# Where the additions of the decode tokens' expert rows stand in VectorE's program

## The chip, the cores and the metric

The kernel runs on one core of a Trainium2 chip. The metric is the device time of one launch in microseconds (us); less is better. Times are medians of several runs; the profile is of one execution more.

## The reference

One inference step of a small hybrid decoder (two layers, model width 1024) for two groups that share the weights: a prompt of 512 tokens and 8 decode tokens with 4096 cached positions each. Layer 0 mixes with differential attention and a gated recurrence, layer 1 with a short gated convolution. After each mixer comes the PEER block, the part that matters here:

```
def one(xb):
    q = (xb @ w_q).reshape(blk, PEER_HEADS, 2, PEER_KDIM // 2)
    s = jnp.einsum('thcd,hcnd->thcn', q, sub_keys).astype(jnp.float32)
    s1, i1 = lax.top_k(s[:, :, 0], PEER_TOPK)
    s2, i2 = lax.top_k(s[:, :, 1], PEER_TOPK)
    cand = (s1[..., :, None] + s2[..., None, :]).reshape(blk, PEER_HEADS, PEER_TOPK * PEER_TOPK)
    sc, ci = lax.top_k(cand, PEER_TOPK)
    ...
    g = jax.nn.softmax(sc, axis=-1)
    act = jax.nn.gelu(jnp.einsum('td,thkd->thk', xb, u_tab[eidx]).astype(jnp.float32))
    coef = (g * act).astype(xb.dtype)
    return jnp.einsum('thk,thkd->td', coef, v_tab[eidx])
```

For each token, 8 heads choose 16 of 128 x 128 = 16384 experts by two top-16 searches over 128 sub-keys each and one over their sums. Each chosen expert has a row in `u_tab` and one in `v_tab`; the output is added to the residual.

## The kernel before

The prompt's 512 tokens lie in four token tiles of 128; the 8 decode tokens are a fifth, `xs[0:DEC, TILES, :]`. Each engine has its own program, written out by hand, and they meet only in semaphores.

PEER is computed in three ways. The decode tokens and token tiles 2 and 3 fetch their experts' rows one by one from HBM (POOL's indirect DMAs into eight `ring` buffers). Token tiles 0 and 1 are computed densely: all 16384 experts in 128 blocks (`NCH`), and a table of gates `G`, which is zero for experts that weren't chosen. A block of gates for 8 tokens (`OT`) and 32 expert blocks (`CH`) is made by TensorE as a product of one-hot matrices: VectorE's `onehots` writes these (lines L1809, L1811 and L1816, called a one-hot group), TensorE's `gates` multiplies them (24 matmuls, L937), ScalarE copies the result into `G` (L1301). One-hot group n waits until TensorE has done gates n - 2, by two buffers.

The search for the experts is `choose`: five stages for each row (MAX8, FIND_INDEX8, MATCH_REPLACE8, MAX8, FIND_INDEX8; L1693 to L1697), for 16 score rows and then for 8 rows of sums, 120 stages in all. A list `beside` of other work is spread among them: one piece after each `every` stages, `every = (5 * 3 * nh) // (len(beside) + 1)`, with nh = 8. After the stages follow L1736 to L1788, which turn places into expert numbers and scores into gates.

In each layer VectorE calls `tile(1)` for token tile 3, then multiplies the decode tokens' fetched u rows, then `tile(2)` (token tile 0), then the additions that this change moves, then `tile(3)` (token tile 1) with one-hot groups 0 to 15 beside it, and `tile(4)` (token tile 2) with groups 16 to 31. Group 0 first waits for `indices_turned`, the copy by ScalarE (L1294, L1295) of what TensorE transposed in `turn(0)` (L927), splits the gates into three bf16 parts (`split_gates`, L1795 and L1797) and copies a table (L1880). At the end `chosen` lets TensorE and POOL into the loops over ranges of experts.

TensorE's order around this is: the last query products (L898); the decode tokens' output rows, gate-weighted sums of the fetched v rows into two PSUM banks (L990, its end is released at L994); `ahead(2)`, products of slices of the u table for the dense tiles (L949, 16 matmuls each; ScalarE's GELU of them is L1310; each slice is loaded into one of two buffers by L566); `turn(0)`; `ahead(1)`; then

```
            pe.wait_ge(dve_bank_free, nv[0])
            for n in range(CH // 2):
                gates(l * NCH + n, n, e2o0, e1o0)
                if n == SCORES_BEHIND:
                    scores(1, q2)
                if n % 4 or n < 8:
                    ahead(1)
            turn(1)
```

`dve_bank_free` counts the additions among other readers of the PSUM banks, and `gates` writes two of these banks. `SCORES_BEHIND` is 11. `turn(1)` waits for the end of `tile(3)`.

Of the kernel before, what the change touches and what calls it, by code (L numbers as in the profile page):

```python
# [22 lines left out]
ALU = mybir.AluOpType  # L23
# [7 lines left out]
TILES = SEQ // P  # L31
DEC = 8
# [206 lines left out]
def program(nc, ins, outs, ctx):  # L239
    def sb(name, shape, dt=F32):  # L240
        return ctx.enter_context(nc.sbuf_tensor(name, shape, dt))

    def sem(name):
        return ctx.enter_context(nc.semaphore(name))


    xs = sb("xs", [P, TILES + 1, D])
# [168 lines left out]
    dve_bank_full, dve_bank_free = sem("dve_bank_full"), sem("dve_bank_free")  # L416
# [992 lines left out]
    def _(dve):  # L1409
        step = Chain(dve, dve_steps)  # L1410
        nv, nn = [0], [0]
        turns = [4, 0]

        def take():
            g = nv[0]
            nv[0] += 1
            dve.wait_ge(dve_bank_full, g + 1)
            k, since = turns
            return ps[4 + (g - since) % k]
# [245 lines left out]
        b = take()  # L1665
# [118 lines left out]
        def gates(r, nh, dst):  # L1784
            v, g = s16[0:r, 0:nh, :], gsum[0:r, 0:nh]
            step(dve.tensor_reduce(g, v, AX.X, ALU.add))
            step(dve.reciprocal(g, g))
            step(dve.tensor_tensor(dst, v, g.unsqueeze(2).broadcast_to([r, nh, TOPK]), ALU.mult))  # L1788

        def split_gates(t):  # L1790


            v = slice(t * P, (t + 1) * P)
            for part in range(3):
                step(dve.tensor_copy(eB[:, 2 + part, v], cfT))  # L1795
                if part < 2:
                    step(dve.tensor_tensor(cfT, cfT, eB[:, 2 + part, v], ALU.subtract))  # L1797
            dve.sem_inc(gates_split, 1)

        def onehots(n, c, e2, e1, hit, pairs, r, tok):  # L1800


            wait_apart(dve, go, gates_in_psum, n + 1)

            def tokens(row, width):
                return eB[:, row, bass.ds(tok, OT)].rearrange("p (a b) -> p a b", b=2).unsqueeze(2)\
                    .broadcast_to([P, OT // 2, width, 2])

            dve.tensor_tensor(hit[c % 2], pairs[:, r * CH:(r + 1) * CH, :].unsqueeze(1).broadcast_to([P, OT // 2, CH, 2]),  # L1809
                              tokens(0, CH), ALU.is_equal).then_inc(dve_steps, 1)  # L1810
            dve.tensor_tensor(e2[c % 2], pairs.unsqueeze(1).broadcast_to([P, OT // 2, P, 2]), tokens(1, P), ALU.is_equal)\  # L1811
                .then_inc(dve_steps, 1)
            step.n += 2
            dve.wait_ge(dve_steps, step.n - 1)
            for part in range(3):
                m = dve.tensor_tensor(e1[c % 2][:, part], hit[c % 2], tokens(2 + part, CH), ALU.mult)  # L1816
                if part < 2:
                    m.then_inc(dve_steps, 1)
            step.n += 2
            m.then_inc(onehots_ready, 1)  # L1820
            dve.wait_ge(dve_steps, step.n)

        def peer(l):
# [8 lines left out]
            b = take()  # L1832
# [5 lines left out]
            def tile(turns, beside=()):  # L1838
                step.clear()
                dve.wait_ge(scores_ready, l * (TILES + 1) + turns + 1)  # L1840

                choose(P, PH, sc, lambda: dve.wait_ge(indices_turned, 1 + l * DT + (turns > 2) + (turns > 3)), beside)
                dve.wait_ge(top_exps_ready, l * (TILES + 1) + turns + 1)
                gates(P, PH, coef.rearrange("p (h k) -> p h k", h=PH))
# [19 lines left out]
            dve.sem_inc(dec_coefs_ready, 1)  # L1864
            tile(2)
            dve.sem_inc(chosen, 1)
            for c in range(2):
                b = take()
                x = xs[0:DEC, TILES, c * 512:(c + 1) * 512]
                dve.tensor_tensor(x, x, b[0:DEC, :], ALU.add).then_inc(dve_bank_free, 1)  # L1870
            dve.wait_ge(dve_bank_free, nv[0])

            def group(n, wait):
                def work():
                    if wait:
                        dve.wait_ge(indices_turned, 1 + l * DT + n * OT // P + 1)
                        dve.wait_ge(queried, l + 1)
                        split_gates(n * OT // P)
                        if n == 0:
                            step(dve.tensor_copy(pairs0, io128.unsqueeze(2).broadcast_to([P, P, 2])))  # L1880
                    onehots(l * NCH + n, n, e2o0, e1o0, hit0, pairs0, 0, n * OT)
                return work

            half = CH // 2
            tile(3, [group(n, n == 0) for n in range(half)])
            dve.sem_inc(chosen, 1)
            tile(4, [group(n, n == half) for n in range(half, CH)])
            keep(0)
# [68 lines left out]
            for t in range(DT):  # L1957
                for h in range(2):
                    x = xs[:, t, h * 512:(h + 1) * 512]
                    step(dve.tensor_tensor(x, x, ps[2 + 2 * t + h][:, :], ALU.add))  # L1960
            dve.sem_inc(dense_sums_taken, 1)
            dve.sem_inc(peer_done, 1)

        peer(0)
        norm(range(DT))

        step(dve.memset(cxp[:, :, 0:SCC - 1], 0.0))
        dve.wait_ge(act_bank_free, A_CG)
        for k in range(KD):
            b = take()  # L1970
            dve.tensor_tensor(cxp[:, k, SCC - 1:SCC - 1 + HALF], b[:, 0:HALF], cgT[:, k, 0:HALF], ALU.mult)\
                .then_inc(dve_bank_free, 1)
            b = take()
# [14 lines left out]
        dve.sem_inc(mixer_steps, 1)  # L1988
        add_out()
        peer(1)  # L1990
        norm(range(DT))

# [89 lines left out]
```

## Time and profile before

| what | value |
|---|---|
| median of 3 timed runs | 3507.42 us (3500.57 to 3509.78) |
| the profiled execution | 3516.04 us, its span 3514.2 us |
| busy share: TensorE matmuls, VectorE, POOL, ScalarE | 90%, 75%, 46%, 11% |
| mean granted TensorE clock | 0.957 |
| the additions, L1870 | 4 in all, two per layer, 0.67 us each |

The span is from the first to the last instruction. The shares are averages over stages that differ: attention (to about 590 us), layer 0's PEER with its choice of experts (about 670 to 990 us) and its loops (to about 1950 us), layer 1's convolution and its PEER the same way (choice from about 2220 to 2545 us).

### The profile page before, as it was taken

What the parts mean: (1) busy time and instruction counts of PE and PEld (TensorE: products, weight loads), DVE (VectorE), ACT (ScalarE), POOL (GpSimd) and SP (SyncE); (2) the same over time, 40 slices, a digit from 0 to 9 for tenths busy, and PEclk for the clock granted to TensorE, in tenths of its full rate; (3) what the DMA queues carried; (4) which work ended last, traced back from release to release, by engine and by line L of the source; (5) the groups of instructions that cost most, each with busy time, mean ns of one, the idle gap of its engine ahead of it and who ended that gap; (6) DMA issues with size and microseconds to landing.
All of it is one profiled execution on the core that took longest, in us unless ns stands there. A gap on an engine that the chain in (4) does not pass through costs nothing.

```text
span 3514.2 us, 56871 instructions
## 1 busy us (share of the span) xinstructions
PE 3166.5 (90%) x17422; PEld 2035.5 (58%) x17422; DVE 2641.7 (75%) x5828; ACT 402.2 (11%) x954; POOL 1628.0 (46%) x1447
## 2 busy tenths in 40 slices
PE   6989898999867899999999899899677999999997
PEld 3452224697733566666656685797533666666654
DVE  5997772196999888888777231487999888888777
ACT  1112112111200000000000100111100100000000
POOL 3756650010047655677666000010077666666664
PEclk9999998999989999999999999999888999999999
DMA  5878986033379999999999327324299999999998
GB/s 202 303 267 313 326 283 188 29 109 115 99 267 401 390 410 410 404 410 410 409 410 410 115 79 64 140 69 143 85 380 397 409 410 410 396 410 410 409 410 333
DMA packets 299980, 1021.62 MB, mean 291 GB/s; under 512 B 57805, under 2 KB 59253, under 8 KB 296638
## 3 DMA queue, kind: packets, MB, share of 16 engines
q0 software_dynamic: 188928, 687.95, 51.0%
q1 hardware_dynamic: 84928, 324.07, 24.1%
q10 hardware_dynamic: 25982, 7.72, 2.4%
q8 instruction: 88, 1.44, 0.2%
q14 instruction: 54, 0.44, 0.0%
HBM read 1013.90 MB, written 5.72 MB: 290 GB/s over the span
## 4 chain that ended last, share of the span: by engine, by line
PE 48%; DMA 19%; DVE 15%; issue 13%; POOL 3%; DVEq 1%; ACT 1%; POOLq 0%; SPq 0%; ACTq 0%; PEldq 0%
PE ps L735 7%; DMA hn<-peer_v_in,area 7%; PE ps L1026 7%; PE ps L1017 6%; PE ps L747 6%; PE ps L898 5%; DMA hn<-peer_u_in,area 5%; PE ps L816 4%; PE ps L949 3%; DMA area<-peer_v_in,area 3%; DMA area<-peer_u_in,area 2%; DVE area L1925 2%; PE ps L937 2%; POOL area L641 2%; PE ps L910 2%
## 5 line engine op out<-in xcount | busy, mean ns | idle before, releaser
L641 POOL DMA_INDIRECT area<-peer_u_in,area x396 | 488.7, 1234 | 901.6 <-DVE area L1925 414.9
L1026 PE MATMUL ps<-area 128*128 128x512 f32 x1600 | 741.4, 606 | 35.3 <-DVE area L1913 35.1
L1017 PE MATMUL ps<-hT,area 128*128 128x256 f32 x3200 | 723.3, 379 | 0.0
L1017 PEld LDWEIGHTS ps<-hT,area 128*128 128x128 f32 x3200 | 608.0, 190 | 168.0 <-issue 95.7
L641 POOL DMA_INDIRECT area<-peer_v_in,area x396 | 458.5, 1158 | 363.1 <-DVE xs L1930 150.9
L1026 PEld LDWEIGHTS ps<-area 128*128 128x128 f32 x1600 | 294.1, 192 | 340.2 <-issue 338.3
L1925 DVE CUSTOM_DVE_ANT_0 area<-area,hn 128x1024 f32<-128x1024 f32 x384 | 455.1, 1224 | 27.4 <-DMA area<-peer_u_in,area 21.6
L937 PE MATMUL ps<-area 128*128 128x32 bf16 x6144 | 192.5, 177 | 115.2 <-DVE area L1816 113.0
L937 PEld LDWEIGHTS ps<-area 128*128 128x128 bf16 x6144 | 186.3, 97 | 188.0 <-issue 162.6
L1930 DVE SCALAR_TENSOR_TENSOR hn<-area,hn 128x1024 f32<-128x1024 f32 x192 | 246.0, 1281 | 46.0 <-DMA area<-peer_v_in,area 42.5
L1930 DVE SCALAR_TENSOR_TENSOR xs<-area,xs 128x1024 f32<-128x1024 f32 x192 | 246.3, 1283 | 41.5 <-DMA area<-peer_v_in,area 27.5
L735 PE MATMUL ps<-area,hT 128*128 128x512 f32 (+1 forms) x560 | 253.0, 612 | 7.6 <-DVEq L1988 5.1
L1301 ACT COPY area<-ps 128x256 f32 (+1 forms) x256 | 95.4, 373 | 1353.5 <-PE ps L937 1293.1
L1042 PE MATMUL ps<-area 128*128 128x512 f32 x448 | 243.8, 695 | 3.9 <-DMA area<-peer_v_in 3.7
L618 POOL DMA_INDIRECT area<-cache_k_in,area x128 | 178.1, 1391 | 141.3 <-DVE area L1506 107.1
L747 PE MATMUL ps<-hT,area 128*128 128x260 f32 x1024 | 226.4, 383 | 2.6 <-PE ps L747 1.8
L747 PEld LDWEIGHTS ps<-hT,area 128*128 128x128 f32 x1024 | 193.9, 190 | 35.2 <-issue 5.3
L816 PE MATMUL ps<-area 128*8 128x512 f32 x412 | 197.9, 621 | 3.8 <-DMA area<-cache_v_in,area 3.5
L735 PEld LDWEIGHTS ps<-area,hT 128*128 128x128 f32 (+1 forms) x560 | 97.2, 176 | 160.3 <-issue 151.1
L1515 DVE TENSOR_TENSOR area<-area,hn 128x1024 f32<-128x1024 f32 x128 | 155.8, 1218 | 39.9 <-ACT hn L1146 19.8
L641 POOL DMA_INDIRECT hn<-peer_v_in,area x132 | 145.6, 1103 | 71.3 <-issue 35.9
L1816 DVE TENSOR_TENSOR area<-area 128x256 bf16<-128x256 bf16 x768 | 177.5, 286 | 0.0
(269 smaller groups left out, 3630.9 us busy)
## 6 DMA issues: line engine op xcount, KB each, us to landing
area<-peer_v_in SPq DMA_DIRECT2D x256, 512.0 KB, 6.7
area<-peer_ut_in SPq DMA_DIRECT2D x200, 512.0 KB, 8.7
area<-wq_in SPq DMA_DIRECT2D x8, 2048.0 KB, 18.7
hn<-peer_ut_in SPq DMA_DIRECT2D x28, 512.0 KB, 3.6
gain<-peer_ut_in SPq DMA_DIRECT2D x28, 512.0 KB, 3.6
area<-w_in_c_in SPq DMA_DIRECT2D x6, 2048.0 KB, 7.5
area<-w_in_a_in SPq DMA_DIRECT2D x5, 2048.0 KB, 11.6
area<-peer_u_in,area POOLq DMA_INDIRECT x396
```

The costliest lines, as they stand in the source:

```text
L618: pool.indirect_dma_start(slot.rearrange("p a c -> p (a c)"), None, ins[cache], bass.IndirectOffsetOnAxis(ap=pgi[:, n:n + 1], axis=0)).the ...
L641: pool.indirect_dma_start(ring[r], None, ins[what + str(l)], bass.IndirectOffsetOnAxis(ap=idx[:, i:i + 1], axis=0)).then_inc(rows_landed[r ...
L735: m = pe.matmul(b[0:rows(t), :], lhs[:, k, cols(t)], w[:, k, :], start=(k == 0), stop=(k == KD - 1))
L747: m = pe.matmul(b[:, 0:HALF], w[:, k, c * P:(c + 1) * P], hT[:, k, half * HALF:(half + 1) * HALF], start=(k == 0), stop=(k == KD - 1))
L816: m = pe.matmul(o[0:8, :], s[:, b_, j * SUB + i, :], vpages[g % len(vpages)][:, i, :], start=False, stop=(j == NG - 1 and i == SUB - 1), s ...
L937: m = pe.matmul(ps[6 + c % 2][:, i * CH:(i + 1) * CH], e2[c % 2][:, i // 2, :, i % 2], e1[c % 2][:, part, i // 2, :, i % 2], start=(part = ...
L1017: m = pe.matmul(ps[c % 2][:, 0:DT * P], us[c][:, k, :], hT[:, k, 0:DT * P], start=(k == 0), stop=(k == KD - 1))
L1026: m = pe.matmul(ps[2 + 2 * t + h][:, :], cT[:, c % 2, t * P:(t + 1) * P], vs[c % 2][:, h * 512:(h + 1) * 512], start=False, stop=False, sk ...
L1042: m = pe.matmul(ps[2 + 2 * t + h][:, :], G[0][:, n, t * P:(t + 1) * P], vs[n % 2][:, h * 512:(h + 1) * 512], start=False, stop=False, skip ...
L1816: m = dve.tensor_tensor(e1[c % 2][:, part], hit[c % 2], tokens(2 + part, CH), ALU.mult)
L1925: m = dve.tensor_tensor_reduce(row, row, hn[:, t, :], 1.0, 0.0, ALU.mult, ALU.add, d16[:, q:q + 1])
L1930: dve.scalar_tensor_tensor(acc[i % 2], row, d16[:, q:q + 1], acc[i % 2], ALU.mult, ALU.add).then_inc(rows_free, 1)
```

## The change

The two additions of the decode tokens' output rows to the residual, and the wait for their end, become a function `add_rows`. It is no longer called between `tile(2)` and `tile(3)`, but is the third piece of work beside `tile(3)`'s search, after one-hot groups 0 and 1. The list has 17 pieces in place of 16.

```
             tile(2)
             dve.sem_inc(chosen, 1)
-            for c in range(2):
-                b = take()
-                x = xs[0:DEC, TILES, c * 512:(c + 1) * 512]
-                dve.tensor_tensor(x, x, b[0:DEC, :], ALU.add).then_inc(dve_bank_free, 1)
-            dve.wait_ge(dve_bank_free, nv[0])
+
+            def add_rows():
+                for c in range(2):
+                    b = take()
+                    x = xs[0:DEC, TILES, c * 512:(c + 1) * 512]
+                    dve.tensor_tensor(x, x, b[0:DEC, :], ALU.add).then_inc(dve_bank_free, 1)
+                dve.wait_ge(dve_bank_free, nv[0])
...
             half = CH // 2
-            tile(3, [group(n, n == 0) for n in range(half)])
+            groups = [group(n, n == 0) for n in range(half)]
+            tile(3, groups[:2] + [add_rows] + groups[2:])
```

## Rows read from the trace of the kernel before

**Rows 1.** The page, part 4: the chain that ended last, shares by engine.

```profile
PE 48%; DMA 19%; DVE 15%; issue 13%; POOL 3%; DVEq 1%; ACT 1%; POOLq 0%; SPq 0%; ACTq 0%; PEldq 0%
```

**Rows 2.** The chain of waits, layer 0: start us, us, what.

```profile
813.73 13.91 PE ps L990 x32
...
887.95 3.46 PE ps L949 x16
...
893.57 1.15 DVE area L1696 x7
```

**Rows 3.** VectorE's timeline, layer 0: start, us, engine, line, operation [idle before, releaser].

```profile
827.75 1.27 DVE L1870 TENSOR_TENSOR xs<-xs,ps 8x512 f32<-8x512 f32 x2 [14.21 <-PEq L994]
829.16 1.45 DVE L1693 MAX8 area<-area 128x8 f32<-128x128 f32 x7
836.55 0.23 DVE L1795 CAST area<-area 128x128 bf16<-128x128 f32 x1 [5.95 <-ACTq L1297]
...
839.99 1.45 DVE L1693 MAX8 area<-area 128x8 f32<-128x128 f32 x7
841.35 0.27 DVE L1809 TENSOR_TENSOR area<-area 128x256 bf16<-128x256 bf16 x1
...
842.75 0.48 DVE L1693 MAX8 area<-area 128x8 f32<-128x128 f32 x2
...
844.45 0.27 DVE L1809 TENSOR_TENSOR area<-area 128x256 bf16<-128x256 bf16 x1
```

**Rows 4.** TensorE's timeline over the same stretch.

```profile
834.90 0.49 PE L927 MATMUL ps<-ident,area 128*128 128x128 f32 x3
836.56 3.72 PE L949 MATMUL ps<-hT,hn 128*128 128x256 f32 x16 [1.16 <-DMA hn<-peer_ut_in]
840.33 0.75 PE L937 MATMUL ps<-area 128*128 128x32 bf16 x24
...
862.38 3.72 PE L949 MATMUL ps<-hT,hn 128*128 128x256 f32 x16 [0.60 <-DMA hn<-peer_ut_in]
...
891.25 1.35 PE L937 MATMUL ps<-area 128*128 128x32 bf16 x48
...
911.81 0.90 PE L927 MATMUL ps<-ident,area 128*128 128x128 f32 x3 [7.38 <-DVEq L1886]
```

**Rows 5.** VectorE's timeline, around one-hot group 14 (at 892.15).

```profile
887.97 0.10 DVE L1695 MATCH_VALUE_LOAD area<-area 128x8 f32 x1
...
892.15 0.29 DVE L1809 TENSOR_TENSOR area<-area 128x256 bf16<-128x256 bf16 x1 [3.71 <-PE ps L937]
...
893.57 1.15 DVE L1696 MAX8 area<-area 128x8 f32<-128x88 f32 x7
...
897.92 0.17 DVE L1736 COPY area<-area 128x8 f32<-128x8 f32 x1
```

**Rows 6.** TensorE's timeline, later in layer 0.

```profile
920.43 6.37 PE L949 MATMUL ps<-hT,gain 128*128 128x256 f32 x16
...
995.07 4.89 PE L1042 MATMUL ps<-area 128*128 128x512 f32 x8
...
1001.22 3.68 PE L1042 MATMUL ps<-area 128*128 128x512 f32 x8
```

**Rows 7.** Windows: us, PE busy (instructions), granted clock, DMA share, GB/s.

```profile
989.00:994.00 5.00, 0.00 (x0) 1.00 0.04 16
994.00:997.50 3.50, 3.07 (x27) 0.52 0.01 2
997.50:1000.00 2.50, 2.46 (x6) 0.99 0.68 208
```

**Rows 8.** VectorE's timeline, layer 1: additions, split, one-hot group 14.

```profile
2378.75 1.27 DVE L1870 TENSOR_TENSOR xs<-xs,ps 8x512 f32<-8x512 f32 x2 [12.91 <-PEq L994]
...
2387.56 0.23 DVE L1795 CAST area<-area 128x128 bf16<-128x128 f32 x1 [5.95 <-ACTq L1297]
...
2444.11 0.29 DVE L1809 TENSOR_TENSOR area<-area 128x256 bf16<-128x256 bf16 x1 [3.29 <-PE ps L937]
```

## The prediction

> **What bounds the kernel now.** I read the page first: the chain that ended last is mostly TensorE [rows 1], but that is a share over the whole program, and the change touches one stretch of some 110 us in each of the two layers. So I then read the chain of waits of that stretch in layer 0 (the reader sees who sets the time, piece by piece) [rows 2], and after it the timelines of VectorE (DVE) and TensorE (PE) over the same microseconds [rows 3 to 5].
>
> From 813.7 to 888 us the chain is PE: the products of the decode rows (L990), then the `ahead` products (L949), one for nearly each block of gates. From about 892 us it is DVE, the last stages of its top-16 search and then the choice of the experts [rows 2]. DVE has two holes before that. It stands 14.21 us before the additions (L1870), until PE has finished the row products, and then 5.95 us before it can split the gates at 836.55, until ScalarE has copied the turned indices [rows 3]. That second hole comes from PE's order: row products, two `ahead` blocks, then `turn(0)` at 834.90 [rows 4], whose copies release DVE. Nothing in that order waits for the additions. Layer 1 has the same two holes, 12.91 and 5.95 us [rows 8].
>
> **The change, part by part.** I work in layer 0; layer 1 runs the same code with the same durations.
>
> 1. *The additions leave the first hole.* `tile(3)` now begins at about 813.6 in place of 829.2. But its first one-hot group needs `indices_turned`, that is `turn(0)` at 834.90 and the copies that end just before 836.55, and this does not move. All DVE can do ahead of it is the stages in front of group 0: seven MAX8 before, six now, since 17 pieces of side work in place of 16 make `every` 120 // 18 = 6 in place of 120 // 17 = 7. They lay in the shadow of the 5.95 us wait anyway. Gain: 0. The 14.21 us become a wait of about 21 us before the split.
>
> 2. *The additions land in front of PE's gates.* PE has `pe.wait_ge(dve_bank_free, nv[0])` before the first `gates`. Before, that was fulfilled at 829, and PE went from its third `ahead` block (ends at 836.56 + 3.72 = 840.28) straight to gates 0 at 840.33 [rows 4]. Now the second addition comes after group 1 and 18 stages. From the end of group 0 at 839.99 [rows 3]: six MAX8 at (841.35 - 839.99) / 7 = 0.194 us are 1.17; group 1 takes 842.75 - 841.35 = 1.40; the six stages to the additions are four MAX8 (0.78) and two FIND_INDEX8. Two MAX8 and five FIND_INDEX8 took 844.45 - 842.75 = 1.70, so one of the latter is (1.70 - 0.39) / 5 = 0.26, two are 0.52. The additions take 1.27, and 0.1 for the wait on their end. Sum: 839.99 + 1.17 + 1.40 + 0.78 + 0.52 + 1.37 = 845.23. **PE stands 4.9 us** where it stood none. Behind its wait are gates 0, all later `ahead` blocks and gates, scores for tile 2, and `turn(1)`; ScalarE's copies and its next slice loads wait on those, and from group 2 on DVE waits for `gates_in_psum`.
>
> 3. *Is the 4.9 us given back?* From group 6 on DVE waits for PE, up to 3.71 us before group 14 [rows 5], and PE waits for no one-hot group up to gates 13 at 891.25. So PE's pace sets group 14, and PE has slack only in its waits for the slices, such as 0.60 us at 862.38 [rows 4]; with two buffers reloaded at the same pace I expect that to stay. If a loader that got 4.9 us of lead kept it, up to about 1 us a layer would come back (estimate from that row). The 7.38 us that PE idles before `turn(1)` at 911.81 [rows 4] are no cover: group 14 comes before them and DVE's tail after it.
>
> 4. *PE's clock.* PE had hardly a pause here. In a later gap of the same layer it ran at granted clock 1.00 (2.4 GHz) through 5.0 us without work, then at 0.52 (1.2 GHz almost throughout) for the next 3.5 us of work [rows 7]; the eight matmuls there took 4.89 us, where 3.68 us is normal [rows 6]: 1.2 us lost. After the longer pause before 920.43, one `ahead` block took 6.37 against 3.72 us [rows 6, 4]: 2.65 us lost. A stall of 4.9 us is on the edge. Bounds 0 and 2.65 us; I take the middle of the two losses, **1.9 us**, as the gap of rows 7 is the nearest row in length. The Trainium skill (TensorE: Matmul & The Clock Gate, Part 1) says that half rate is the default and that activity lifts it, so that an idle engine falls back; by that rule the loss is certain, and the two layers pay 17.4 us in place of the 13.6 us without it. The trace agrees that such a fall exists, in rows 7.
>
> 5. *The side work ends earlier in the search.* Group 14 used to start at stage 105 of 120 and now starts at 96, group 15 at 102 in place of 112. When group 14 is held by PE, DVE has nine more stages behind it than before: eight MATCH_REPLACE8, 0.21 us each (887.97 to the end of the next at 888.18), and one MAX8, 1.15 / 7 = 0.16 us [rows 5]. **1.9 us** are added after group 14. Bound: none if DVE reached group 14 late by itself; it does not, as it idles 3.71 us there and will idle longer.
>
> 6. *Behind it.* The end of `tile(3)` sets `chosen`, PE's `turn(1)`, all of `tile(4)` and the start of the loops, all of them in the chain. ScalarE's exponentials come after its last `ahead` result and are needed some 13 us after stage 120; they fit. POOL has its eight first rows under way and waits for DVE. So the delay passes whole.
>
> Group 14 moves from 892.15 to 892.15 + 4.9 + 1.9 = 898.95, and L1736 from 897.92 to 897.92 + 4.9 + 1.9 + 1.9 = 906.6. **Sum: 8.7 us a layer, 17.4 us in all.** The profiled execution took 3516.04 us, 1.8 more than its span of 3514.2, so it would become 3533.4; it stood 8.6 above the median of the three timed runs, 3507.42. The same 17.4 us on that median give 3524.8.
>
> **Rivals.**
> - *Faster: the first hole closes and the time comes off.* DVE's 14.21 + 12.91 = 27.1 us of waiting disappear and `tile(3)` ends so much earlier: 3480.3 us. It decides if group 0 could run before 828 us, that is if `turn(0)` were ahead of the row products. The Trainium skill (Perfetto Trace Analysis, Optimization Strategy) says to look for the gaps of the engine that matters and let what fills them start sooner; that would speak for this outcome. Against it: rows 3 and 4, the second wait of 5.95 us ends with ScalarE, not with the additions.
> - *No change: DVE absorbs PE's stall.* If DVE's own work, not PE's, set group 14, only the additions' 1.3 us a layer would be paid: 3507.42 + 2.6 = 3510. For it: DVE is over nine tenths busy up to group 6. Against it: 3.71 and 3.29 us idle before group 14 in the two layers [rows 5, 8].
> - *Slower without the clock's part.* The stall is too short to drop the clock: 2 x (4.9 + 1.9) = 13.6 us, 3521.0.
>
> **How the numbers follow.** The forecast (stall, clock and tail) has 0.55, the same without the clock 0.20, absorbed 0.15, faster 0.06; 0.04 is left for what I do not see. 0.3% is 10.5 us, about what a measurement of this kernel can tell from no change; the three runs spread over 9 us by themselves. Of the two slower cases (0.75) a few hundredths may measure under 10.5 us: slower 0.71, same 0.22, faster 0.07. The range goes from the absorbed case, 3510, up to the forecast with the larger clock loss (2 x (4.9 + 2.65 + 1.9) = 18.9, 3526.3) and 4 us of scatter: 3530.
>
> **What the profile will show.** DVE: no wait before L1870, but some 20 us before L1795, whose start stays at about 836.5 (part 1). PE: a wait of about 4.9 us before the first L937 in each layer, released by DVE L1870 or the sequencer's wait (part 2). Granted clock 0.50 in part of 845 to 852, and one L949 block of 5 us or more (part 4). The wait before the 15th L1809 grows from 3.7 to some 9 us, less whatever the earlier groups wait (part 3), and 24 stages follow its start (part 5). I am wrong if L1795 starts earlier, if gates 0 still start at 840, or if L1736 does not move by 7 to 9.5 us.

## The result and the profile after

The changed kernel is slower: 3529.25 us median of 6 runs (3523.15 to 3532.45) against 3508.6 us of 6 runs of the kernel before; ratio 1.0057, 95% interval 1.0041 to 1.0072, that is 14 to 25 us. Its profiled execution took 3529.66 us, with a span of 3527.8 us. The shares of the engines are as before, and the chain's shares nearly so (DMA 18% in place of 19%):

```profile
span 3527.8 us, 56873 instructions
...
PE 48%; DMA 18%; DVE 15%; issue 13%; POOL 3%; ACT 1%; DVEq 1%; POOLq 0%; SPq 0%; ACTq 0%; PEldq 0%
```

So the page doesn't show the change; the timelines do. VectorE's, layer 0 (the additions are L1872 in the changed kernel; columns as in [rows 3]):

```profile
812.11 1.26 DVE L1693 MAX8 area<-area 128x8 f32<-128x128 f32 x6 [0.23 <-DVE area L1788]
834.91 0.23 DVE L1795 CAST area<-area 128x128 bf16<-128x128 f32 x1 [21.54 <-ACTq L1297]
...
838.34 1.25 DVE L1693 MAX8 area<-area 128x8 f32<-128x128 f32 x6
...
842.21 1.25 DVE L1872 TENSOR_TENSOR xs<-xs,ps 8x512 f32<-8x512 f32 x2
...
898.13 0.29 DVE L1809 TENSOR_TENSOR area<-area 128x256 bf16<-128x256 bf16 x1 [4.05 <-PE ps L937]
...
902.72 1.29 DVE L1696 MAX8 area<-area 128x8 f32<-128x88 f32 x8
...
905.80 0.17 DVE L1736 COPY area<-area 128x8 f32<-128x8 f32 x1
```

The two waits of before, 14.21 and 5.95 us [rows 3], have become one of 21.54 us with the same end: ScalarE's copy of the turned indices. Nothing was gained by starting the search early. TensorE's timeline over the same stretch:

```profile
833.26 0.49 PE L927 MATMUL ps<-ident,area 128*128 128x128 f32 x3
834.88 3.72 PE L949 MATMUL ps<-hT,hn 128*128 128x256 f32 x16 [1.13 <-DMA hn<-peer_ut_in]
843.77 0.80 PE L937 MATMUL ps<-area 128*128 128x32 bf16 x24 [5.16 <-DVE xs L1872]
844.41 6.06 PE L949 MATMUL ps<-hT,gain 128*128 128x256 f32 x16
850.31 0.76 PE L937 MATMUL ps<-area 128*128 128x32 bf16 x24
...
919.68 0.90 PE L927 MATMUL ps<-ident,area 128*128 128x128 f32 x3 [9.27 <-DVEq L1889]
```

The wait of 5.16 us before gates 0 is new; before, gates 0 followed the third `ahead` block at once [rows 4]. The block behind it takes 6.06 us where 3.70 us is normal. The windows say why (us, PE busy, granted clock, DMA share, GB/s):

```profile
838.70:841.00 2.30, 0.00 (x0) 1.00 0.41 68
841.00:842.00 1.00, 0.00 (x0) 1.00 0.77 311
842.00:843.70 1.70, 0.00 (x0) 0.61 0.08 34
843.70:849.00 5.30, 5.23 (x35) 0.50 0.00 0
849.00:850.00 1.00, 1.00 (x6) 0.90 0.00 0
```

PE's last block before the pause ends at 838.60. The granted clock was 1.00 (2.4 GHz) until 842.00 and fell to 0.50 (1.2 GHz) before 843.70, still in the pause. PE then worked for 5.3 us at 0.50 before it rose. And the chain of waits now runs through the additions (start, us, what):

```profile
840.91 0.85 DVE area L1693 x4
841.76 0.53 DVE area L1694 x2
842.30 1.18 DVE xs L1872 x2
843.77 0.80 PE ps L937 x24
844.57 5.92 PE ps L949 x16
```

**Where the time went.** TensorE's two L927 (`turn(0)` and `turn(1)`) are marks that every kernel has (L929 in the last one); the distance between their starts measures the stretch that the change touches, apart from the scatter elsewhere. Before, the first two stood at 834.90 and 911.81 us [rows 4] and those of layer 1 at 2385.91 and 2463.76; after, at 833.26 and 919.68, and 2393.27 and 2478.57.

| stretch | before | after | difference |
|---|---|---|---|
| start to `turn(0)`, layer 0 | 834.90 | 833.26 | -1.6 |
| `turn(0)` to `turn(1)`, layer 0 | 76.91 | 86.42 | +9.5 |
| from there to `turn(0)`, layer 1 | 1474.10 | 1473.59 | -0.5 |
| `turn(0)` to `turn(1)`, layer 1 | 77.85 | 85.30 | +7.4 |
| from there to the end | 1050.4 | 1049.2 | -1.2 |

The two stretches give +17.0 us, all the rest -3.4 us. The distances are those of one profiled execution each. The medians say 20.7; both this and 17.0 lie inside the interval of 14 to 25 us.

### The profile page after: what moved, and what is told of

Read it like the earlier page. It is cut to its first block, busy times and chain, and to the rows that moved or that the text cites. A ratio compares the mean times of both kernels' runs of the same rounds, so it can differ in the third digit from the quotient of the medians.

```text
span 3527.8 us, 56873 instructions
## 1 busy us (share of the span) xinstructions
PE 3165.1 (90%) x17422; PEld 2041.2 (58%) x17422; DVE 2642.6 (75%) x5828; ACT 401.7 (11%) x954; POOL 1614.0 (46%) x1447
## 4 chain that ended last, share of the span: by engine, by line
PE 48%; DMA 18%; DVE 15%; issue 13%; POOL 3%; ACT 1%; DVEq 1%; POOLq 0%; SPq 0%; ACTq 0%; PEldq 0%
DMA hn<-peer_v_in,area 8%; PE ps L1026 7%; PE ps L735 7%; PE ps L1017 7%; PE ps L747 6%; PE ps L898 5%; DMA hn<-peer_u_in,area 5%; PE ps L816 4%; PE ps L949 4%; DMA area<-peer_u_in,area 3%; DVE area L1928 2%; POOL area L641 2%; PE ps L937 2%; PE ps L910 2%; DMA area<-peer_v_in,area 1%
## 5 line engine op out<-in xcount | busy, mean ns | idle before, releaser
L641 POOL DMA_INDIRECT hn<-peer_v_in,area x132 | 145.7, 1104 | 72.6 <-issue 31.4
L898 PE MATMUL ps<-hT,area 128*128 128x128 f32 x1536 | 178.2, 281 | 0.0
```

What stands on the lines that cost most here:

```text
L641: pool.indirect_dma_start(ring[r], None, ins[what + str(l)], bass.IndirectOffsetOnAxis(ap=idx[:, i:i + 1], axis=0)).then_inc(rows_landed[r ...
L898: m = pe.matmul(b[:, c * P:c * P + P], wqs[g][:, k, c * P:(c + 1) * P], hT[:, k, cols(t)], start=(k == 0), stop=(k == KD - 1))
```

## The experiments

The theory, A, has three terms for each layer: PE stands before gates 0 until the additions are done; its clock falls in the stall; and the 17th piece makes the groups denser, so that more search is left behind the last group that PE holds up. The rivals are B, VectorE is the bound and the additions are simply paid once they are out of its hole, and C, the denser groups are the whole cost. Measured, with the distance in layers 0 and 1:

| kernel | median, us | ratio to before (interval) | distances, us |
|---|---|---|---|
| before | 3507 to 3510 | | 76.9, 77.9 |
| changed | 3529.25 | 1.0057 (1.0041 to 1.0072) | 86.4, 85.3 |
| spacing only | 3511.17 | 1.0011 (1.0002 to 1.0020) | 79.1, 78.4 |
| additions in the wait | 3508.62 | 0.9998 (0.9989 to 1.0008) | 76.8, 75.8 |
| additions with group 1 | 3524.7 | 1.0046 (1.0033 to 1.0059) | 83.7, 83.2 |
| no stall | 3514.11 | 1.0013 (1.0004 to 1.0022) | 78.7, 78.9 |
| a block in the stall | 3515.87 | 1.0020 (1.0008 to 1.0032) | 81.0, 80.9 |
| ten useless matmuls in it | 3531.46 | 1.0061 (1.0045 to 1.0077) | 86.3, 87.2 |
| five of them | 3523.15 | 1.0044 (1.0029 to 1.0058) | 83.5, 82.7 |
| search first, 88 stages | 3510.71 | 1.0002 (0.9993 to 1.0012) | 77.6, 79.6 |
| the same, scores later | 3504.38 | 0.9985 (0.9974 to 0.9995) | 72.3, 76.0 |
| 80 stages, scores later | 3499.4 | 0.9979 (0.9967 to 0.9992) | 72.6, 71.7 |
| three blocks later too | 3479.15 | 0.9918 (0.9906 to 0.9931) | 62.6, 61.8 |

The distance of one and the same order scatters by up to 2 us with PE's waits for the slices of the u table: 77.9 and 75.8 us in layer 1 for before and for the additions in the wait. So where a term has a wait or a block of its own in TensorE's timeline, that is the better measure of it.

**The spacing alone.** The kernel before with an empty piece:

```
-            tile(3, [group(n, n == 0) for n in range(half)])
+            groups = [group(n, n == 0) for n in range(half)]
+            tile(3, groups[:2] + [lambda: None] + groups[2:])
```

> The additions stay between tile(2) and tile(3); only an empty 17th piece stands where the change has the additions, so that the pieces come after every 6 stages in place of 7. My theory (A) has three terms per layer: PE's stall before gates 0 (5.1 us), its clock afterwards (2.3 us), and DVE's longer tail behind one-hot group 14 (1.9 us). By A this kernel pays the tail alone: the distance from turn(0) to turn(1), 76.9 and 77.9 us before, becomes 78.8 and 79.8, no wait before gates 0, in all +3.8 us. Rival B (DVE is the bound, and what is moved out of its hole is paid): 0 us. Rival C (the denser groups are the whole cost): +9.5 and +7.4 us in the two layers, about +20 us in all.

Measured: +3.9 us by the ratio (0.0011 x 3508; the interval goes from 0.7 to 7 us), +2.2 and +0.5 us in the distances, which scatter as much as that. PE's wait before `turn(1)`, for VectorE's last stages and its choice of experts, is steadier:

```profile
912.24 0.90 PE L927 MATMUL ps<-ident,area 128*128 128x128 f32 x3 [9.27 <-DVEq L1887]
```

It is 9.27 and 9.26 us in the two layers, where it was 7.38 and 7.37 [rows 4]: 1.9 us more in each, as worked out. It has this length in every kernel with 17 evenly spread pieces, and 7.4 to 7.7 us in those with 16. The tail is real; C is out.

**The additions inside the wait.** The changed kernel, with

```
-            tile(3, groups[:2] + [add_rows] + groups[2:])
+            first_group = groups[0]
+            groups[0] = lambda: (add_rows(), first_group())
+            tile(3, groups)
```

> The additions run beside the search, but as the first thing of group 0's piece, ahead of its wait for the turned indices; spacing 7 as before. They should stand right after the row products (DVE is then idle in any case). By A nothing is gained or lost: distance 76.9 and 77.9 us, the kernel of before within its scatter, though DVE no longer stands before tile(3). If the hole of 14.2 and 12.9 us before the additions is worth anything, L1736 of tile(3) comes earlier and up to 27 us are gained. By B also 0.

Measured: no difference. VectorE, layer 0:

```profile
811.39 1.45 DVE L1693 MAX8 area<-area 128x8 f32<-128x128 f32 x7 [0.23 <-DVE area L1788]
824.22 1.27 DVE L1872 TENSOR_TENSOR xs<-xs,ps 8x512 f32<-8x512 f32 x2 [11.37 <-PEq L994]
833.08 0.23 DVE L1795 CAST area<-area 128x128 bf16<-128x128 f32 x1 [7.59 <-issue]
```

The search starts before the additions here too, and no stall of PE follows; still nothing is gained. The 27 us of waiting before the additions were worth nothing by themselves. That answers the faster rival of the prediction.

**The additions with group 1, spacing as before.**

```
+            second_group = groups[1]
+            groups[1] = lambda: (second_group(), add_rows())
+            tile(3, groups)
```

> The additions stay where the change puts them (behind one-hot group 1) but share its piece, so that the spacing is 7 as before. By A: stall of PE before gates 0 of 1.36 + 1.40 + 1.3 = 3.8 us, then 1.5 to 2.3 us by the lower clock if it falls in so short a stall, no longer tail: distance +5.3 to +6.1 us a layer, +11 to +12 us in all (+7.6 if the clock stays). Rival B: +1.3 us a layer. Rival C: 0.

Measured: +16 us, distances +6.8 and +5.3. PE, layer 0:

```profile
842.60 0.80 PE L937 MATMUL ps<-area 128*128 128x32 bf16 x24 [4.31 <-DVE xs L1872]
843.24 5.87 PE L949 MATMUL ps<-hT,gain 128*128 128x256 f32 x16
```

A stall of 4.31 us (3.8 expected) and a block that is 2.2 us longer make 6.5 us: stall and clock without the tail (the wait before `turn(1)` is 7.37 us, as before). B, which allows 1.3 us a layer, is out.

**No stall.** The changed kernel; the row products go to banks that the gates don't write, and the wait moves behind the gates:

```
             pe.wait_ge(dec_coefs_ready, l + 1)
+            take_turns(4)
             b0, b1 = vbank(), vbank()
...
-            pe.wait_ge(dve_bank_free, nv[0])
             for n in range(CH // 2):
...
             pe.wait_ge(chosen, (l + 1) * (TILES + 2))
+            pe.wait_ge(dve_bank_free, nv[0])
...
             def add_rows():
+                turns[:] = [4, nv[0]]
```

> The changed kernel, but the row products go to PSUM banks 4 and 5 in both layers, which the gates don't use, and PE's wait for the additions stands before the dense sums in place of before gates 0. By A the stall and the clock's part go and the tail stays: distance 78.8 and 79.8 us, +3.8 us against the kernel of before, 17 us less than the changed kernel. Rival B: +2.6 us or more. Rival C: as slow as the changed kernel, +20 us.

Measured: +4.6 us by the ratio. The additions stand behind group 1 as in the changed kernel, and 15 us are gone with PE's wait.

**A useful block in the stall.** In TensorE's and ScalarE's programs alike:

```
             turn(0)
-            ahead(1)
+            ahead(2)
...
-                if n % 4 or n < 8:
+                if n % 4 or n < 4:
```

> The changed kernel, with one ahead block more before PE's wait for the additions, and none behind gates 4 in its place, so that as many blocks as before stand ahead of gates 12. By A PE works through its stall: it loses 4.9 - 3.6 = 1.3 us in place of 4.9, the clock stays at 1.00, and the tail of 1.9 us remains: distance from turn(0) to turn(1) +3.2 us a layer, +6.4 us in all. If the stall did not cost because PE stands, but because DVE does its work in another order, it stays as slow as the changed kernel, +20 us.

Measured: +7 us by the ratio, as expected, but not in the parts expected. PE, layer 0:

```profile
841.05 0.77 PE L937 MATMUL ps<-area 128*128 128x32 bf16 x24 [1.94 <-DVE xs L1872]
841.66 5.31 PE L949 MATMUL ps<-hT,hn 128*128 128x256 f32 x16
```

The stall left over is 1.94 us, not 1.3, and the clock, expected at 1.00, fell all the same: the block lost 1.6 us. Stall, clock and tail make 5.4 us; the distances grew by 4.1 and 3.1 us. In layer 1 the wait was 2.46 us and the block took 5.39. The rest came back where PE waits for slices: behind gates 0 it waits for none in this run, 0.86 and 1.82 us in the two layers before.

**Useless work in the stall.** The changed kernel with, before the wait:

```
+            pe.wait_ge(dve_bank_free, nv[0] - 2)
+            for _ in range(10):
+                pe.matmul(ps[7][:, :], ones[:, :], hT[:, 0, 0:SEQ], start=True, stop=True)
             pe.wait_ge(dve_bank_free, nv[0])
```

> The changed kernel, with ten 512-column matmuls of no use (4.3 us, into bank 7, whose content nobody reads) in PE's stall before gates 0. The output is the same. The stall by itself stays, only the clock has no reason to fall. By A the block behind gates 0 takes 3.7 in place of 6.0 us and the distances are 2.3 us shorter than in the changed kernel: 84.1 and 83.0 us, 4.7 us less in all, +16 us against before. If the clock is no part of the cost: the changed kernel's time.

I mis-sized it: in the trace ten float32 matmuls of 512 columns are 20 instructions and took 8.75 us, so gates 0 started 13.67 us after `turn(0)` in place of 10.51. Though gates 0 came 3.2 us later (3.3 in layer 1), the distance was the same as in the changed kernel in layer 0 and 1.9 us longer in layer 1. What came back is the clock: the block behind gates 0 took 3.70 us in both layers. The rest of the difference lies in PE's waits for slices, 0.6 us shorter in layer 0 and 0.9 us longer in layer 1. But the run mixes two sizes. Repeated with five:

> The run with useless matmuls in PE's stall again, with five in place of ten: ten took 8.75 us and held gates 0 up by 3.2 us. Five should take 4.4 us of the 5.1 us stall. By A the block behind gates 0 takes 3.7 in place of 6.06 us, the distance from turn(0) to turn(1) is 2.3 us shorter than in the changed kernel (84.1 and 83.0 us), the time 4.7 us shorter, about 3524. If the lower clock is no part of the cost, 86.4 and 85.3 us and the changed kernel's time.

Measured: 3523.15 us, distances 83.5 and 82.7. PE's timeline, then the windows:

```profile
843.56 4.46 PE L1000 MATMUL ps<-hT,ones 128*128 128x512 f32 x10
849.12 0.75 PE L937 MATMUL ps<-area 128*128 128x32 bf16 x24 [1.10 <-DVE xs L1875]
849.72 3.70 PE L949 MATMUL ps<-hT,gain 128*128 128x256 f32 x16
```

```profile
838.00:842.00 4.00, 3.10 (x16) 1.00 0.60 196
842.00:846.00 4.00, 4.00 (x14) 1.00 0.27 54
846.00:850.00 4.00, 2.90 (x30) 1.00 0.24 97
```

Gates 0 still wait for the additions and start 10.50 us after `turn(0)`, as in the changed kernel (10.51); the clock stays at 1.00, the block takes 3.70 us, and the distances shrink by 2.9 and 2.6 us. Of this the block itself is 2.4 and 2.3 us: the price of the clock, apart from the stall's. The rest is within the scatter of the distances.

**Search first.** If the search can't gain by starting early, more of it can run in the hole. `choose` got explicit places for its pieces, and the additions one where the row products are just done:

```
+                        while beside and count[0] >= places_of_work[0]:
+                            places_of_work.pop(0)
+                            beside.pop(0)()
...
+            tile(3, [add_rows] + groups, [64] + [88 + 2 * n for n in range(half)])
```

> DVE's hole filled with what can fill it: tile(3)'s search runs 88 stages before group 0 (the additions are its piece at stage 64, when the row products are just done), then a group after every second stage. About 20 us of search lie in what were 14.2 + 6 us of waiting. By A the groups stay bound to PE's pace (group 14 is held by gates 12), so only what lies behind group 14 shrinks, from 15 stages to 4: 2.9 - 0.9 = 2.0 us a layer, 4 us in all, about 3505 us. If DVE were the bound, the 15 to 18 us moved into the hole would come off in each layer.

Measured: no difference; a miss of 5 us. PE, layer 0:

```profile
837.41 0.75 PE L937 MATMUL ps<-area 128*128 128x32 bf16 x24 [1.68 <-issue]
838.02 5.39 PE L949 MATMUL ps<-hT,gain 128*128 128x256 f32 x16
```

88 stages were too many here. VectorE reached its split of the gates without any wait, but at 833.66, 3.2 us after `turn(0)` at 830.46, where the copies allow it after 1.65 us (836.55 - 834.90 [rows 3, 4]). So PE stood 1.68 us before gates 0, its clock fell, and the block took 1.7 us more: 3.4 us lost against a tail 2.0 us shorter (5.44 us before `turn(1)` in place of 7.38). In layer 1 the wait was 2.37 us and the block took 5.07. About 20 us of search moved into the hole took no more off the end than those 2.0 us; the rest of it stays with PE's pace.

**Scores later**, `SCORES_BEHIND = 13` in place of 11, then with 80 stages ahead of group 0 (`[64] + [80 + 38 * n // 15 for n in range(half)]`):

> As the kernel that searches first, with PE's scores for token tile 2 (3.7 us) moved from behind gates 11 to behind gates 13 (SCORES_BEHIND 13). By A they then come off the path to group 14: another 3.6 us a layer, distance 76.9 - 5.6 = 71.3 and 72.2 us, 11 us in all, about 3498 us. If PE's pace did not set the end of tile(3), no change against the kernel that searches first.

> Search first, scores later, but 80 stages ahead of group 0 in place of 88: with 88 DVE came 1.5 us late to the split, PE stood 1.7 us before gates 0 and the clock fell. By A the split starts again when ScalarE's copy allows it, no wait and no low clock at gates 0, and distance 76.9 - 3.6 - 1.4 = 71.9 us in both layers (the last limit is then ScalarE's exponentials behind its last ahead result), 10 us in all: about 3499 us, 5 us less than with 88. If the short wait did not matter: as with 88 stages, 3504 us.

Measured: 3504.38 us, 6 us above what was expected, mostly since layer 1 (76.0 us) still had a wait of 2.23 us before gates 0 and a block of 5.18 us behind it. Layer 0 had a wait of 0.30 us only, though up to gates 11 this is the order of the run before, which waited 1.68 us there: with 88 stages VectorE has nothing to spare, and whether it is late differs between executions. Then 3499.4 us and 72.6 and 71.7 us with 80 stages, as expected. VectorE waits again for the copy, 1.26 us, and PE hardly at all:

```profile
832.32 0.23 DVE L1799 CAST area<-area 128x128 bf16<-128x128 f32 x1 [1.26 <-ACTq L1297]
```

```profile
836.08 0.75 PE L937 MATMUL ps<-area 128*128 128x32 bf16 x24 [0.19 <-issue]
836.68 3.70 PE L949 MATMUL ps<-hT,gain 128*128 128x256 f32 x16
```

**Three `ahead` blocks later as well**, with ScalarE's exponentials of `tile(3)` before its last `ahead` result:

```
+FIRST_HALF = (0, 1, 3, 4, 6, 7, 9, 10, 13, 14, 15)
+SECOND_HALF = (17, 18, 19, 21, 22, 23, 25, 26, 27, 28, 29, 30, 31)
...
             turn(1)
+            ahead(1)
             for n in range(CH // 2, CH):
                 gates(l * NCH + n, n, e2o0, e1o0)
-                if n % 4 and n < CH - 1:
+                if n in SECOND_HALF:
```

> As that one, with three of the eleven ahead blocks that stand before gates 12 moved behind turn(1) (one before gates 16, two at the end, where PE idles 4.3 and 12.7 us), and ScalarE's exponentials of tile(3) before its last ahead result. If PE's order of work is what sets the end of tile(3) (A), 3 x 3.55 = 10.6 us come off it: distance about 61 us, and since tile(4) is bound by DVE the loops start some 16 us earlier in each layer: 3474 to 3480 us. If the order does not matter because PE's total work is the limit, no gain against the run with 80 stages.

Measured: 3479.15 us, 0.82% faster than the kernel before and 1.4% faster than the changed one. The wait before `turn(1)`, 7.38 us before [rows 4], is nearly gone in layer 0 (in layer 1 it is 2.04 us):

```profile
886.57 3.70 PE L951 MATMUL ps<-hT,gain 128*128 128x256 f32 x16
890.68 0.55 PE L929 MATMUL ps<-ident,area 128*128 128x128 f32 x3 [0.41 <-DVEq L1899]
891.07 3.62 PE L951 MATMUL ps<-hT,hn 128*128 128x256 f32 x16
```

This is the strongest evidence that the order of work sets the stretch: no work was taken out, and 28 us came off. Against the run with 80 stages the distances shrink by 10.0 and 9.9 us, where three blocks make 10.6. Two things are not told apart. ScalarE's exponentials were moved in the same run, and no run has only the blocks or only the exponentials moved. And the early search is a part of it. In the kernel before, VectorE waited 9.1 us for PE between the split and group 14, which came 57.3 us after `turn(0)`, so without its waits it could not have come before 48.2; here it comes at 44.7. An estimate from these numbers: without the early search some 3.5 us of layer 0's gain would be missing.

## Why the prediction was right

By its own steps; predicted 3524.8 us, +17.4. The traces give +17.0 and the medians +20.7. That the sum meets the traces within 0.4 us is in part luck: layer 0 lost 9.5 us and layer 1 7.4, where I had counted 8.7 for both.

1. *The additions leave the first hole: 0.* Right. The split starts 1.65 us after `turn(0)` in both kernels (834.91 - 833.26 and 836.55 - 834.90), and the wait before it is 21.54 us, where I had said about 21.
2. *PE stands 4.9 us.* Right: 5.16 and 5.29 us. The additions end 10.20 us after `turn(0)`, as worked out (10.23); the 0.2 us too little lie in the step from their end to PE's start (843.46 to 843.77), for which I had counted 0.1. What I had wrong is that PE stood none before in both layers. In layer 1 it stood 0.84 us already, so the stall adds only 4.5 us there:

```profile
2391.33 0.75 PE L937 MATMUL ps<-area 128*128 128x32 bf16 x24 [0.84 <-issue]
```

3. *Not given back.* Right for layer 0: behind gates 0, PE's waits for slices come to 0.83 us after and 0.86 before. In layer 1 they went from 1.82 us at two blocks to nothing of note, more than the 1 us that I had allowed. With the 0.84 us of point 2, and 0.6 us the other way by which the first block behind `turn(0)` came later, this is why that layer lost 7.4 and not 9.5 us. Whether the stall's lead did it or scatter stays open: in one layer these waits come to 0 to 2.0 us in the kernels without a long stall and to 0 to 1.5 us in those with one. I also read the chain too simply. I called it PE from 813.7 to 888 us, but it passes three times through the load of a slice, 14.0 us in all, so PE's pace stood close to that of the loads. Two of the three:

```profile
857.61 4.73 DMA hn<-peer_ut_in
870.81 4.98 DMA gain<-peer_ut_in
```

4. *The clock, 1.9 us.* Right in kind, somewhat small: the blocks lost 2.4 and 2.3 us, and with five useless matmuls they lost nothing. I took the middle of 1.2 and 2.65 us; the upper end was nearer. The Trainium skill's rule (TensorE: Matmul & The Clock Gate, Part 1), by which an idle engine falls back to half rate, agrees with the windows of the changed kernel (0.61 on average from 842.00 to 843.70 us, 0.50 from there to 849.00).
5. *The tail, 1.9 us.* Right: from group 14 to L1736 5.77 us before (897.92 - 892.15 [rows 5]) and 7.67 after (905.80 - 898.13); the run with the spacing alone has 1.9 us in each layer in the wait before `turn(1)`.
6. *The delay passes whole.* Right: the stretches between the marks changed by -1.6, -0.5 and -1.2 us.

One sign came out otherwise than its figure: the wait before group 14 did not grow to about 9 us but to 4.05. I had allowed for waits of earlier groups, but not for how many: with the groups denser, DVE reaches each of them sooner, and its waits for PE stand before groups 3 to 10 and group 14. They add up to 16.9 us, 9.1 before. It changes nothing in the sum. Of the signs of being wrong, L1736 was to move by 7 to 9.5 us: it moved by 7.9 us on the clock of the trace, and by 9.5 and 7.5 us in the two layers if counted from `turn(0)`.

Of the rivals, "faster" was refuted by the additions in the wait, "absorbed" (3510 us) by the result itself and by the additions with group 1, and "no clock" by the windows.

## What to carry to other kernels

A wait is worth no more than what the same engine waits for next: VectorE stood 14 us before the additions, but its next wait, on another engine, ended when it did before. When an instruction moves later, look for who waits for it; here two additions of 0.67 us held the engine that set the pace, for 5.2 us, and its lower clock added 2.4. In such a stretch the gain lies in the order of the engine that sets the pace. Filling the other engine's hole gave nothing by itself; it took the moving of one group of scores and 3 of the 28 blocks behind the point that others wait for, with the hole filled, to gain 28 us.

## What was not expected of the hardware

- Short pauses can cost clock too. Before gates 0, the five waits of 1.68 to 2.46 us in three runs were each followed by a block of 5.07 to 5.39 us in place of 3.70; behind waits of up to 1.10 us it took 3.70. The wait of 1.68 us thus cost 3.4 us. The clock fell only when PE was at work again: in that run it was 1.00 until 838.00, 0.6 us after gates 0 began, and 0.50 from 838.60.
- But the length of a pause doesn't decide it alone. In the last kernel a wait of 1.35 us before gates 13 was followed by slow scores in layer 0 (5.45 us) and not in layer 1 (3.82 us), and in the kernel before a wait of 3.16 us, in layer 1's loops, kept the clock at 1.00 (the eight matmuls behind it took 3.68 us, the normal time). What decides it no run here isolates. Lines of the last kernel, then of the one before:

```profile
872.49 0.75 PE L939 MATMUL ps<-area 128*128 128x32 bf16 x24 [1.35 <-DVE area L1825]
873.09 5.45 PE L921 MATMUL ps<-area 128*128 128x128 f32 x32
2409.93 0.75 PE L939 MATMUL ps<-area 128*128 128x32 bf16 x24 [1.35 <-DVE area L1825]
2410.53 3.82 PE L921 MATMUL ps<-area 128*128 128x128 f32 x32
```

```profile
2572.46 0.75 PE L937 MATMUL ps<-area 128*128 128x32 bf16 x24 [3.16 <-DVE area L1816]
2573.06 3.68 PE L1042 MATMUL ps<-area 128*128 128x512 f32 x8
```

- Matmuls whose result nobody reads, put into a stall that was there in any case, kept the clock up: the block behind it took 3.70 us in place of 6.06 and 6.00. Ten of them, longer than the stall, gave this back by starting gates 0 some 3.2 us later.
- A float32 matmul of 512 columns is two instructions in the trace and took about 0.88 us at full clock (8.75 us for ten).
